# Delta-rule stage: heads in pairs, other work between a level's two products, and a new order on four engines

## The reference, cut to what matters

```python
A = jnp.where(strict, jnp.einsum('bhnid,bhnjd->bhnij', k_beta, k) * dmask, 0.0)
T = lax.linalg.triangular_solve(eye + A, jnp.broadcast_to(eye, A.shape), left_side=True, lower=True)
u = T @ v_beta
w = T @ (k_beta * jnp.exp(decay)[..., None])
qk = jnp.einsum('bhnid,bhnjd->bhnij', q, k) * dmask
...
v_new = u_n - w_n @ S
o_n = qd_n @ S + qk_n @ v_new
S = S * gl_n[..., None, None] + jnp.einsum('bhck,bhcv->bhkv', kd_n, v_new)
```

## Time and profile before

| | |
|---|---|
| median of 3 runs | 1417.9 us (1417.83 to 1418.61) |
| profiled execution, its own time | 1418.34 us |
| span of its instructions | 1416.6 us |
| busy: PE, PE's weight loads | 1365.3 us (96%), 1243.7 us (88%) |
| busy: DVE, ACT, POOL | 948.4 (67%), 590.8 (42%), 569.3 us (40%) |
| DMA | 234.64 MB, mean 166 GB/s |
| granted clock of TensorE, mean | 0.989 |

### The profile page before, as it was taken

How to read it: one execution, slowest core, us unless ns; L and a number is a source line. 1 busy time by engine, 2 the same in 40 slices (tenths; PEclk the granted TensorE clock), 3 DMA queues, 4 the chain that set the end, 5 groups by cost and what they waited for, 6 DMA issues and landing times.

```text
span 1416.6 us, 29230 instructions
## 1 busy us (share of the span) xinstructions
PE 1365.3 (96%) x10652; PEld 1243.7 (88%) x10652; DVE 948.4 (67%) x1593; ACT 590.8 (42%) x1455; POOL 569.3 (40%) x645
## 2 busy tenths in 40 slices
PE   6999899989989999999999999999999999999997
PEld 4899899988978888888799999999999997887675
DVE  6517786774366666788879656666666567576388
ACT  6524344345566656525544333333333325443220
POOL 4887857771033434233331443432443434000051
PEclk8999999999999999999999999999999999999999
DMA  9431435335364545432133454554444448997794
GB/s 345 124 107 42 113 101 134 104 88 152 98 217 132 164 134 166 139 124 75 67 105 105 135 175 145 163 187 159 131 152 157 149 154 331 357 373 255 266 326 173
DMA packets 184409, 234.64 MB, mean 166 GB/s; under 512 B 17708, under 2 KB 118640, under 8 KB 184304
## 3 DMA queue, kind: packets, MB, share of 16 engines
q1 hardware_dynamic: 180128, 221.36, 48.3%
q10 hardware_dynamic: 4176, 11.89, 2.1%
HBM read 170.29 MB, written 61.73 MB: 164 GB/s over the span
## 4 chain that ended last, share of the span: by engine, by line
PE 61%; DVE 7%; ACT 4%; issue 3%; POOL 1%; DMA 1%; SPq 0%; POOLq 0%; DVEq 0%; ACTq 0%
PE bank L2350 30%; PE bank L2264 11%; PE bank L305 3%; PE bank L1674 2%; PE bank L1128 2%; PE bank L1137 2%; PE bank L1634 2%; PE bank L2281 1%; PE bank L1139 1%; PE bank L1170 1%; ACT hp L1724 1%; PE bank L1161 1%; DVE stat L1757 1%; ACT vp L1275 1%; DVE xt L1792 1%
## 5 line engine op out<-in xcount | busy, mean ns | idle before, releaser
L2264 PE MATMUL bank<-split 128*128 128x512 f32 x924 | 212.3, 390 | 3.0 <-DVE split L2397 2.3
L2264 PEld LDWEIGHTS bank<-split 128*128 128x128 f32 x924 | 172.7, 188 | 44.8 <-DVE split L2393 5.2
L2350 PE MATMUL bank<-Tlo,rh 128*128 128x272 f32 x640 | 184.7, 289 | 0.0
L2350 PE MATMUL bank<-Thi,rh 128*128 128x272 f32 x640 | 184.2, 288 | 0.0
L2350 PE MATMUL bank<-Thi,rl 128*128 128x272 f32 x640 | 184.0, 288 | 0.0
L305 PE MATMUL bank<-hT_hi,whi 128*128 128x384 f32 (+1 forms) x504 | 166.7, 331 | 2.4 <-DVE wlo L295 2.2
L305 PE MATMUL bank<-hT_hi,wlo 128*128 128x384 f32 (+1 forms) x504 | 164.9, 327 | 0.0
L305 PE MATMUL bank<-hT_lo,whi 128*128 128x384 f32 (+1 forms) x504 | 164.8, 327 | 0.0
L2350 PE MATMUL bank<-hT_lo,rh 128*128 128x272 f32 x480 | 138.5, 289 | 0.0
L2350 PE MATMUL bank<-hT_hi,rl 128*128 128x272 f32 x480 | 138.4, 288 | 0.0
L2350 PE MATMUL bank<-hT_hi,rh 128*128 128x272 f32 x480 | 137.9, 287 | 0.0
(11 more groups left out here) (450 smaller groups left out, 3358.3 us busy)
## 6 DMA issues: line engine op xcount, KB each, us to landing
wada<-w_ada SPq DMA_DIRECT2D x12, 2048.0 KB, 9.1
raw<-w_up SPq DMA_DIRECT2D x40, 512.0 KB, 5.0
wsum<-w_down SPq DMA_DIRECT2D x11, 1024.0 KB, 5.6
wt<-wsum SPq DMA_DIRECT2D x11, 1024.0 KB, 4.0
rW<-wt SPq DMA_DIRECT2D x44, 256.0 KB, 6.6
split<-split SPq DMA_DIRECT2D x22, 512.0 KB, 5.2
wraw<-w_in SPq DMA_DIRECT2D x21, 512.0 KB, 4.4
rows<-convrow ACTq DMA_DIRECT2D x16, 577.5 KB, 3.7
```

Of the source, the lines that this page charges most:

```text
L2264: last = pe.matmul(ps[down_bank(q, r)][:], a[:, rows], w, start=(k == 0 and m == 0), stop=(k == KH - 1 and m == 2))
L2350: last = pe.matmul(ps[banks[c]][:, 0:NC], w[:, ks], a, start=(n < 3 and k == 0 and p == 0), stop=(k == 3 and p == 2), skip_group_check=True)
```

## The change

TensorE: `level` is split into `level_P` (first products) and `level_X` (second products), and other work is put between them in halves: read_state in level 0, gram(n) by pairs of heads in and after level 1, turn_q(n) in and after level 2, turn_o(t-1) in and after level 3, turn_v(n) in and after level 4, ada_columns(t-1) in level 5. `state` is split into `read_state`, `new_values` and `outputs`; turn_A(n) goes between the two halves of the outputs, and scores(n) behind them. Two heads share a PSUM bank (pair p in bank p), so keep_P, keep_V and grow_X work on two heads at once, and the semaphores g_P, g_Pb, g_X, g_XX, g_Vb count pairs. k S and V lie in banks 2 and 3.

ScalarE: squares_q(n) moves from level 2 to behind keep_A(n); v_scaled stands before whole_X and keep_V, keep_A behind them; decay is split (differences by pairs in levels 0 and 2, the row factors at the end of the tile). VectorE: right_sides moves to behind growth 0, out_rows from behind growth 1 to behind growth 2, coupling(n) from behind growth 4 to behind growth 5; new_state goes ahead of first_blocks, keep_scores behind later_levels. GpSimd: scales is split into scales_k and scales_q, the output's scale takes three steps instead of five (the factor of q goes into the epsilon), q_decayed(t) runs behind out_scale(t-1). SyncE: one wait's count. In the last tile ScalarE also waits for q_decayed (g_qd) before the levels. The arithmetic is the same but for that regrouping of the output's scale.

The diff, cut to its core:

```diff
+        kS_of = lambda h: ps[2][:, h * P:(h + 1) * P]
+        V_of = lambda h: ps[2 + h // 2][:, h % 2 * P:(h % 2 + 1) * P]
+        kv_of = lambda h: ps[h // 2][:, h % 2 * P:(h % 2 + 1) * P]
...
+            def gram(n, p):
...
+            def level_P(t, l):
...
-                    pe.wait_ge(on["g_R"], t * HEADS)
-                    pe.wait_ge(on["g_S"], t * HEADS)
-                for h in range(HEADS):
+                for p in range(PAIRS):
                     if l:
-                        pe.wait_ge(on["g_X"], lv(t, l - 1, h) + 1)
-                    if l == LV - 1:
-                        last = pe.matmul(ps[h][DOWN, 0:HB], Lc[x][UP, l, h, :], Xc[x][UP, h, 0, :], start=True, stop=True)
-                    else:
+                        pe.wait_ge(on["g_X"], lvp(t, l - 1, p) + 1)
+                    elif t:
+                        pe.wait_ge(on["g_S"], (t - 1) * HEADS + 2 * p + 2)
+                    for i, h in enumerate((2 * p, 2 * p + 1)):
+                        if l == LV - 1:
+                            last = pe.matmul(p_at(p, DOWN, i), Lc[x][UP, l, h, :], Xc[x][UP, h, 0, :], start=True, stop=True)
+                            continue
                         for q in (UP, DOWN):
-                            last = pe.matmul(ps[h][q, 0:HB], Lc[x][q, l, h, :], Xc[x][q, h, 0, :], start=True, stop=True)
+                            last = pe.matmul(p_at(p, q, i), Lc[x][q, l, h, :], Xc[x][q, h, 0, :], start=True, stop=True)
                     last.then_inc(on["g_P"], 1)
...
+            def level_X(t, l):
+
+                x = t % 2
+                for p in range(PAIRS):
+                    pe.wait_ge(on["g_Pb"], lvp(t, l, p) + 1)
+                    for i, h in enumerate((2 * p, 2 * p + 1)):
...
-            def state(t):
-                x, st = t % 2, state_of(t)
+            def read_state(t):
                 if t == 0:
                     pe.wait_ge(on["g_init"], 5)
                 if t == PTILES:
                     pe.wait_ge(on["s_state"], 32)
                 for h in range(HEADS):
-                    pe.wait_ge(on["g_X"], lv(t, top(t), h) + 1)
-                    pe.matmul(hb(h, 0), stg[:, x, k_ + h, :], Sst[:, st, h, :], start=True, stop=True).then_inc(on["g_kS"], 1)
+                    if t:
+                        pe.wait_ge(on["g_S"], (t - 1) * HEADS + h + 1)
+                    pe.matmul(kS_of(h), stg[:, t % 2, k_ + h, :], Sst[:, state_of(t), h, :], start=True, stop=True).then_inc(on["g_kS"], 1)
+
+            def new_values(t):
                 pe.wait_ge(on["g_Xf"], since("g_Xf", t + 1))
+                pe.wait_ge(on["g_R"], t * HEADS + HEADS)
                 for h in range(HEADS):
-                    pe.wait_ge(on["g_R"], t * HEADS + h + 1)
-                    pe.matmul(hb(h, 3), Xf[x][:, h, :], Rb[:, h, :], start=True, stop=True).then_inc(on["g_V"], 1)
+                    pe.wait_ge(on["g_X"], lvp(t, top(t), h // 2) + 1)
+                    pe.matmul(V_of(h), Xf[t % 2][:, h, :], Rb[:, h, :], start=True, stop=True).then_inc(on["g_V"], 1)
+
+            def outputs(t, heads):
...
+                for h in heads:
+                    pe.wait_ge(on["g_Vb"], t * PAIRS + h // 2 + 1)
                     pe.matmul(h4(4)[:, h, :], qd[x][:, h, :], Sst[:, st, h, :], start=True, stop=False)
                     pe.matmul(h4(4)[:, h, :], QK[x][:, h, :], Vb[:, h, :], start=False, stop=True)
-                    pe.matmul(hb(h, 1), kdec[x][:, h, :], Vb[:, h, :], start=True, stop=True).then_inc(on["g_kv"], 1)
...
                 n, more = t + 1, t + 1 < TILES
-                level(t, 0)
+                level_P(t, 0)
+                read_state(t)
+                level_X(t, 0)
                 if more:
-                    turn_kq(n)
-                level(t, 1)
-                level(t, 2)
+                    turn_k(n)
+                level_P(t, 1)
+                if more:
+                    gram(n, 0)
+                level_X(t, 1)
+                if more:
+                    gram(n, 1)
+                level_P(t, 2)
+                if more:
+                    turn_q(n, FIRST2)
+                level_X(t, 2)
+                if more:
+                    turn_q(n, LAST2)
+                level_P(t, 3)
                 if t:
-                    turn_o(t - 1)
-                level(t, 3)
+                    turn_o(t - 1, FIRST2)
+                level_X(t, 3)
+                if t:
+                    turn_o(t - 1, LAST2)
+                level_P(t, 4)
                 if more:
-                    scores(n)
-                level(t, 4)
+                    turn_v(n, FIRST2)
+                level_X(t, 4)
                 if more:
-                    gram(n)
+                    turn_v(n, LAST2)
+                    level_P(t, 5)
                 if t:
                     ada_columns(t - 1)
                 if more:
-                    level(t, 5)
+                    level_X(t, 5)
+                new_values(t)
+                outputs(t, FIRST2)
+                if more:
                     turn_A(n)
-                    turn_v(n)
-                state(t)
+                outputs(t, LAST2)
+                if more:
+                    scores(n)
                 if t < PTILES:
...
             def keep_P(t, l):
                 rows = DOWN if l == LV - 1 else slice(0, P)
-                for h in range(HEADS):
-                    act.wait_ge(on["g_P"], lv(t, l, h) + 1)
-                    act.activation(Pb[rows, h, 0:HB], ps[h][rows, 0:HB], ACT.Copy).then_inc(on["g_Pb"], 1)
+                for p in range(PAIRS):
+                    act.wait_ge(on["g_P"], lvp(t, l, p) + 1)
+                    act.activation(Pb[rows, pair(p), 0:HB], ps[p][rows, 0:P].rearrange("p (h c) -> p h c", c=HB),
+                                   ACT.Copy).then_inc(on["g_Pb"], 1)
...
             def keep_V(t):
-                for h in range(HEADS):
-                    act.wait_ge(on["g_V"], t * HEADS + h + 1)
-                    act.activation(Vb[:, h, :], hb(h, 3), ACT.Copy).then_inc(on["g_Vb"], 1)
+                for p in range(PAIRS):
+                    act.wait_ge(on["g_V"], t * HEADS + 2 * p + 2)
+                    act.activation(Vb[:, pair(p), :], ps[2 + p][:, 0:2 * P].rearrange("p (h c) -> p h c", c=P), ACT.Copy).then_inc(on["g_Vb"], 1)
...
                 if more:
                     keep_P(t, 0)
+                    decay_diff(n, FIRST2)
                     keep_P(t, 1)
                     squares_k(n)
                     keep_P(t, 2)
+                    decay_diff(n, LAST2)
+                    decay_exp(n)
+                    keep_P(t, 3)
+                    k_decayed(n)
+                    keep_P(t, 4)
+                    keep_P(t, 5)
+                    v_scaled(n)
+                    whole_X(t)
+                    keep_V(t)
+                    keep_A(n)
                     squares_q(n)
-                    keep_P(t, 3)
-                    decay(n)
-                    keep_P(t, 4)
-                    decay_exp(n)
-                    k_decayed(n)
-                    keep_P(t, 5)
-                    whole_X(t)
-                    keep_A(n)
-                    v_scaled(n)
-                    keep_V(t)
                     squares_o(t)
+                    decay_row(n)
                     continue
                 tile_hi(act, 0, 0)
                 act.wait_ge(on["g_X0"], 2 * TILES)
                 act.wait_ge(on["g_QK"], TILES)
+                act.wait_ge(on["g_qd"], TILES)
...
-                    scales(t + 1)
-                    q_decayed(t + 1)
-                    causal(t + 1)
+                    q_decayed(t)
+                if n < TILES:
+                    scales_k(n)
+                    causal(n)
+                    scales_q(n)
...
-                for h in range(HEADS):
-                    dve.wait_ge(on["g_XX"], lv(t, l, h) + 1)
+                for p in range(PAIRS):
+                    dve.wait_ge(on["g_XX"], lvp(t, l, p) + 1)
+                    src = ps[p][:, P:3 * P].rearrange("p (h x c) -> p h x c", h=2, x=2)
+                    if l == LV - 1:
...
-                    dve.tensor_tensor(Xc[x][:, h, lo:2, :], Xc[x][:, h, lo:2, :], src[:, lo:2, :], ALU.add).then_inc(on["g_X"], 1)
+                    dve.tensor_tensor(Xc[x][:, pair(p), lo:2, :], Xc[x][:, pair(p), lo:2, :], src[:, :, lo:2, :], ALU.add).then_inc(on["g_X"], 1)
...
                 grow_X(t, 0)
+                right_sides(t)
                 if not more:
                     wo_low(dve, 0)
                 grow_X(t, 1)
-                if t:
-                    out_rows(t - 1)
                 if not more:
                     wo_low(dve, 1)
                 grow_X(t, 2)
+                if t:
+                    out_rows(t - 1)
                 if not more:
                     wo_low(dve, 2)
                 grow_X(t, 3)
@@ -1552,21 +1613,19 @@
                 if not more:
                     wo_low(dve, 4)
                 if more:
```

(58 more changed lines are left out.)

117 lines of the change are left out of this document (61 added, 56 removed).

## The result

The changed kernel takes 1455.5 us (median of 4 runs, 1454.09 to 1457.09), the kernel before 1418.0 beside it: ratio 1.0264, 95% interval 1.0246 to 1.0282. The forecast of slower was right; its size was not: 1443, range 1433 to 1453, so 12.5 us short and 2.5 outside. The profiled execution took 1457.09 us, its span is 1455.4, 38.8 more than before.

What follows compares the result with a forecast made beforehand. TensorE's own order was taken to bound the delta stage. Middle tiles +19.6, tile 0 +2.5, last tile +3.4 and -0.5 ahead of the stage gave +25 on the profiled 1418.3, so 1443 us, range 1433 to 1453.

Steps and rivals of the forecast that it cites:

- Part 1: Fillers between a level's products: size changes cost +2.2 us a tile, removed waits give -1.85.
- Part 2: Four new waits in TensorE's order: 0.25, 0.6, 0.3 (outputs for keep_V of a pair) and 1.3 us.
- (a): turn_o's first half waits for out_rows, now behind level 2's adds: 0.25 us.
- (d): scores, behind the outputs, waits for squares_q, which is moved behind keep_A: 1.3 us.
- the middle tile: Tiles 1 to 7: +2.8 us each, level 0's first loads 25.3 us apart instead of 22.5.
- VectorE's 0.5: Before the next tile's X0, new_state now precedes first_blocks: 0.5 us, hidden inside (d)'s 1.3.
- Rival 1: Half of (d) is cover, ScalarE finishing keep_A and squares_q sooner: 1437 us; chance 0.10.
- rival 5: Copies and adds of pairs dearer than 0.30 and 0.43, 0.1 to 0.2 a level: 1450 us; chance 0.11.
- Tile 0: First tile: no turn_o or ada_columns, so (a) goes and (b) is 1.5 instead of 0.6: +2.5 us.
- the last tile: Few fillers, loop set by VectorE and ScalarE; right_sides, out_rows, q_decayed wait, longer pair chain: about +3.4 us (bounds 1 to 5).
- Rival 2: New waits drop TensorE's clock, each tile losing 1 to 2 us more: 1451 to 1459 us; chance 0.08.
- (b): new_values waits for whole_X, which stands behind v_scaled on ScalarE: 0.6 us.

Runs made afterwards that it cites:

- whole fillers: The kernel with both edits, with gram, turn_q, turn_o and turn_v each unsplit between a level's two products: 1447.2 us, ratio 1.0187.
- the kernel with both edits: The changed kernel with whole_X ahead of v_scaled and squares_q between the copies of levels 4 and 5, both on ScalarE: 1436.2 us, ratio 1.0117.
- the filler in (b): The changed kernel with three unused 128x128 products between level 5 and new_values in every tile but the last: 1445.1 us, ratio 1.0189.
- the filler in (d): The changed kernel with five unused 128x128 products between the outputs and scores: 1457.9 us, ratio 1.0274.
- (b) shortened: The changed kernel with whole_X ahead of v_scaled on ScalarE again, nothing else: 1445.5 us, ratio 1.0183.
- (d) gone: The changed kernel with squares_q moved from behind keep_A to between the copies of levels 4 and 5: 1443.7 us, ratio 1.0164.
- VectorE's order is changed on top: The kernel with both edits, with out_rows behind growth 1 and first_blocks, first_level ahead of new_state: 1435.1 us, ratio 1.0122.
- the last 0.34 us filled: The kernel with both edits and VectorE's order changed, plus one unused 128x128 product ahead of new_values: 1430.6 us, ratio 1.0082.

## Why the prediction was right and wrong

- Part 1, size changes at 0.20 out and 0.15 or 0.09 in: right. The filler between level 2's products costs what was said (482.87 to 483.48 is 0.61, of which 0.47 are the loads), and the whole fillers gave 24.83 for 24.8.
- Part 2, (a) to (d): right within 0.1 each (0.22, 0.69, 0.36, 1.34), and so the middle tile at full clock: 25.38 for 25.3. VectorE's 0.5 was hidden and came out as 0.39 (1.23 less 0.84) when (d) was gone. Rival 1 and rival 5 did not happen.
- Tile 0 and the last tile: the last is 20.23 at full clock in the kernel with both edits, +3.3 for a forecast of +3.4, most of it level 0 (2.3, read_state's loads and the wait for q_decayed) and right_sides (0.85); a fall added 1.7. Tile 0 was forecast at +2.5 and took +5.7. Of that the fall behind new_values is 1.2 (3.78 from new_values to turn_A against 2.58 at full clock), and its level 0 at the lower clock takes 4.89 against 3.39 in the kernel with whole fillers, where the clock there is 1.00; before it took 3.83. The rest of tile 0's +5.7 stays open.
- Rival 2, the clock: this is the step that failed. The sum has no term for it: it was given 0.08 and mostly left out of the range, "waits of up to 0.5 and ada_rows' gaps leave the clock at 1.00 in the tile". Those rows showed no wait behind thin work: before, TensorE had full-size transposes between level 5 and its wait. After, (b) alone is 0.69 and stands right behind ada_columns and half-array products. The falls took 7.5 us in the middle tiles, 1.2 in tile 0 and 1.7 in the last, 10.4 of the 13.8 by which the profiled span's growth missed the forecast. The price in a tile that fell (1 to 2 us) was right (1.3 to 1.6). That the result (1455.5) lies inside the rival's 1451 to 1459 is in part luck: it had all tiles fall, five of seven did, and it looked to (d) first, where filling the wait changed nothing. The Trainium skill (TensorE: Matmul & The Clock Gate, Part 1) says that a gate sets TensorE's clock by how busy it has been of late; the filler in (b) agrees, with 25.40 in every middle tile, while the filler in (d) shows that it matters where TensorE is kept busy.

What is open: why two of seven equal tiles keep the clock. Equal tiles with equal waits fall or not, and edits change which and how many: five in the changed kernel, six with (d) filled, two with (b) shortened or (d) gone, one with both, three when the fillers are whole or VectorE's order is changed on top, one again with the last 0.34 us filled. Each count is from one profiled execution. Of the kernels in the new order only the one with (b)'s 0.69 filled had none in its middle tiles. Open too are the 1.0 us behind the stage.

## What to carry to other kernels

Price a wait with what stands before it: behind narrow and half-array products a wait of 0.69 us on TensorE came with falls of 1.3 to 1.6 us in five of seven tiles, and three products without a use in that wait ended them at no cost of their own. A step that runs in the shadow of another engine's chain is free where it is; move it out and it is paid in full (0.90 here), unless the chain is shortened with it. And the chain named step by step before the change (turn_A, keep_A, squares_q, scores) came out within a tenth of a microsecond; the surprises lay in what had no row yet.

## What was unexpected of the hardware

- TensorE's granted clock fell to 0.50 (520.0 to 522.0) in a tile that is busy 93% of the time (24.84 of 26.70), with 0.79 us of idling just ahead as the longest of that place. A wait of 1.26 us behind full-size products was followed by no fall in the changed kernel or with (b) filled, nor one of 1.12 with (b) shortened.
- A fall costs by what it meets: 1.3 us where it covers new_values and half of the outputs (pair of loads 0.55 for 0.30).
